# A two-layer hybrid decoder step on one core: norm sums taken token by token, a page-sum copy moved ahead of page issues, and attention heads with blocks turned one or two ahead of the scores

## What is computed

```python
def l2norm(x):
    xf = x.astype(jnp.float32)
    return xf * lax.rsqrt(jnp.sum(xf * xf, axis=-1, keepdims=True) + EPS)

# fox_prompt, for each block of 128 queries
s = jnp.einsum('bqhd,bkhd->bhqk', qi, k).astype(jnp.float32) * scale
s = s + ci[..., :, None] - cT[:, :, None, :]
s = jnp.where(kpos[None, :] <= qpos[:, None], s, -jnp.inf)
p = jax.nn.softmax(s, axis=-1).astype(v.dtype)
return jnp.einsum('bhqk,bkhd->bqhd', p, v)

# fox_sample: 2048 past tokens per sample, in 16 pages of 128
return (jnp.einsum('bhqk,bkhd->bqhd', p[..., :P], vp)
        + jnp.einsum('bhqk,bkhd->bqhd', p[..., P:], v))

# gdn_mix
c, conv_new = causal_conv(conv_in, conv_prev, conv_w)
c = jax.nn.silu(c)
q = l2norm(q.reshape(Bn, L, GDN_HEADS, GDN_DK)) * GDN_DK ** -0.5
k = l2norm(k.reshape(Bn, L, GDN_HEADS, GDN_DK))
...
o, S_new = run_chunks(gdn_chunk, S0.astype(jnp.float32), (q, k, v, g, beta), GDN_CHUNK)
o = rmsnorm(o, norm_g) * jax.nn.silu(z.reshape(...))
```

## Time and profile before

| | us |
|---|---|
| median of 3 runs | 2619.35 |
| lowest, highest | 2618.45, 2621.92 |
| the profiled execution's own time | 2619.68 |
| its span | 2617.9 |
| mean granted clock of TensorE, as a share of full speed | 0.977 |

### The profile page before, as it was taken

How to read it: one execution, slowest core, us unless ns; L and a number is a source line. 1 busy time by engine, 2 the same in 40 slices (tenths; PEclk the granted TensorE clock), 3 DMA queues, 4 the chain that set the end, 5 groups by cost and what they waited for, 6 DMA issues and landing times.

```text
span 2617.9 us, 53417 instructions
## 1 busy us (share of the span) xinstructions
PE 2497.5 (95%) x20047; PEld 2395.9 (92%) x20047; DVE 1269.6 (48%) x2225; ACT 566.7 (22%) x847; POOL 1682.8 (64%) x750
## 2 busy tenths in 40 slices
PE   7999998997789899999999999999999899999997
PEld 7999998995467799999999999999889799999996
DVE  4444335786333564443344443366766644444433
ACT  3222101004633222220022220022222221222101
POOL 5777775663411377777777777765545457777773
PEclk9999999998789899999999999999999999999998
DMA  4333334894375333333323333233333423333331
GB/s 125 90 89 96 101 79 113 285 308 131 84 220 188 85 89 95 89 88 99 118 81 89 95 91 100 82 91 100 116 116 98 126 81 88 89 95 90 96 93 61
DMA packets 472390, 291.19 MB, mean 111 GB/s; under 512 B 32785, under 2 KB 438411, under 8 KB 472270
## 3 DMA queue, kind: packets, MB, share of 16 engines
q1 hardware_dynamic: 407286, 221.15, 29.0%
q10 hardware_dynamic: 64992, 68.54, 8.4%
HBM read 273.50 MB, written 16.23 MB: 111 GB/s over the span
## 4 chain that ended last, share of the span: by engine, by line
PE 83%; DVE 8%; ACT 3%; issue 3%; DMA 1%; POOL 1%; ACTq 1%; DVEq 0%; SPq 0%; POOLq 0%
PE ACC L799 72%; PE ACC L1055 2%; PE ACC L1028 1%; DVE TB L2261 1%; DMA SSR<-in_state_ret_S 1%; DVE SSR L2178 1%; POOL WLO L708 1%; PE ACC L1306 0%; PE ACC L1296 0%; DVE XL L1736 0%; PE ACC L1122 0%; PE ACC L1037 0%; POOL WHI L705 0%; PE ACC L893 0%; PE ACC L1330 0%
## 5 line engine op out<-in xcount | busy, mean ns | idle before, releaser
L705 POOL TENSOR_TENSOR WHI<-RAW,ZERO 128x1024 fp32r<-128x1024 f32 (+1 forms) x341 | 693.0, 2032 | 677.2 <-PE ACC L799 640.3
L708 POOL TENSOR_TENSOR WLO<-RAW,WHI 128x1024 fp32r<-128x1024 f32 (+1 forms) x341 | 915.5, 2685 | 49.3 <-POOL WHI L705 2.3
L799 PE MATMUL ACC<-XH,WHI 128*128 128x260 f32 x4032 | 822.6, 285 | 4.3 <-DVE XL L1736 2.0
L799 PE MATMUL ACC<-XH,WLO 128*128 128x260 f32 x4032 | 813.7, 283 | 0.0
L799 PE MATMUL ACC<-XL,WHI 128*128 128x260 f32 x4032 | 812.4, 283 | 0.0
L799 PEld LDWEIGHTS ACC<-XH,WHI 128*128 128x128 f32 x4032 | 624.8, 189 | 22.9 <-issue 6.5
L799 PEld LDWEIGHTS ACC<-XH,WLO 128*128 128x128 f32 x4032 | 622.9, 189 | 0.0
L799 PEld LDWEIGHTS ACC<-XL,WHI 128*128 128x128 f32 x4032 | 621.6, 189 | 0.0
L799 PE MATMUL ACC<-HH,WHI 128*128 128x260 f32 x1408 | 284.2, 283 | 1.1 <-POOL WLO L708 1.1
L799 PE MATMUL ACC<-HH,WLO 128*128 128x260 f32 x1408 | 283.1, 282 | 0.0
L799 PE MATMUL ACC<-HL,WHI 128*128 128x260 f32 x1408 | 282.6, 282 | 0.0
(11 more groups left out here) (391 smaller groups left out, 2398.7 us busy)
## 6 DMA issues: line engine op xcount, KB each, us to landing
RAW<-in_ffn_w_gu SPq DMA_DIRECT2D x176, 512.0 KB, 3.9
RAW<-in_ffn_w_down SPq DMA_DIRECT2D x64, 704.0 KB, 4.8
KPAGES<-in_cache_fox_k ACTq DMA_DIRECT2D x128, 256.0 KB, 4.1
RAW<-in_c_w_in SPq DMA_DIRECT2D x48, 512.0 KB, 3.9
VPAGES<-in_cache_fox_v SPq DMA_DIRECT2D x72, 256.0 KB, 3.1
RAW<-in_ab_w_in SPq DMA_DIRECT2D x28, 512.0 KB, 5.4
VPAGES<-in_cache_fox_v ACTq DMA_DIRECT2D x56, 256.0 KB, 3.3
SSR<-in_state_ret_S ACTq DMA_DIRECT2D x8, 1024.0 KB, 5.4
```

Of the source, the lines that this page charges most:

```text
L705: pool.tensor_tensor(WHI[:, slot, 0:nk, :], RAW[:, slot, 0:nk, :], ZERO[:, :].broadcast_to([P, nk, P]), ALU.add).then_inc(hi_split, 1)
L708: pool.tensor_tensor(WLO[:, slot, 0:nk, :], RAW[:, slot, 0:nk, :], WHI[:, slot, 0:nk, :].bitcast(F32), ALU.subtract).then_inc(split, 1)
L799: ins = pe.matmul(ACC[acc][:, n, 0:HALF], w[:, slot, k, :], a[:, k0 + k, n * HALF:(n + 1) * HALF], start=first and opens, stop=final and c ...
```

## The change

1. **Attention heads.** Turns of blocks 0 and 1 of head h come before the first score of head h+1, and each later turn(h, q+2) right behind values(h, q), ahead of score(h+1, q+1). The turn of the next head's values into tokens (`vtok`) goes behind these turns. ACT takes both first turned blocks at once, takes exponents of two blocks together, puts exp(h, 3) into head h, and copies the value bank of head h only in head h+1, behind the next query copy; DVE's `lo` moves likewise. The four silus of the last head go behind all taps.
2. **Norm sums token by token.** The squares of a chunk of 128 tokens become the weights, and one column of ones is streamed: the sum of each token comes out on its own partition, in 5 columns a head (four chunks of 128 tokens and one that covers the last 128, 8 of them new). So there are 40 matmuls of one column for q and k, and 20 for the output norm. Root and reciprocal work on 128 x 20 or 128 x 40. `over_partitions` spreads them back with the column broadcast as weights against the identity: six matmuls for each of 8 (and 4) heads. `ROWSEL` goes. DVE squares q, ACT squares k in two parts; `SQH` lies elsewhere. Three of the four `values()` stand ahead of the sums.
3. **Page sum.** `value_sum(1)` stands ahead of `sample_gates()` and the page issue on ACT, and corner_xt(1) directly behind corner_xt(0) on PE.

```diff
@@ fox heads, PE
             for h in range(FOX_HEADS):
-                if 0 < h < FOX_HEADS - 1:
-                    fox_tokens(h + 1)
+                later = 0 < h < FOX_HEADS - 1
+                if later:
+                    fox_token_turn(h + 1, AB_K, "ktok")
+                fox_turn(h, 0)
+                fox_turn(h, 1)
+                if later:
+                    fox_token_turn(h + 1, AB_V, "vtok")
                 for q in range(NBLK):
-                    fox_turn(h, q)
                     if h + 1 < FOX_HEADS:
                         score(h + 1, q)
...
                     fox_values(h, q)
-
-            pe.wait_ge(fb_dve.sem, fb_dve.value("lo", FOX_HEADS - 1))
+                    if q + 2 < NBLK:
+                        fox_turn(h, q + 2)
+
@@ fox heads, ACT
             for h in range(FOX_HEADS):
-                if 0 < h < FOX_HEADS - 1:
-                    fox_query(h + 1)
-                    fox_keys(h + 1)
-                for q in range(NBLK):
-                    fox_turned(h, q)
-                    if h + 1 < FOX_HEADS:
-                        exponent(h + 1, q)
-                    if q < NBLK - 1:
-                        conv_taps(3 * h + q)
-                    if h == FOX_HEADS - 1:
-                        part = channels(GQ + 2 * q, 2)
-                        if q == 0:
-                            act.wait_ge(cs_pool.sem, cs_pool.value("a3"))
-                        act.wait_ge(cv_pool.sem, cv_pool.value("add3", 2 * q + 1))
-                        act.activation(part, part, ACT.Silu).then_inc(cv_act, 1)
-                await_step(act, fb_pe, "pv3", h)
-                fb_act.done(act.activation(MOH[:, h, 0:SEQ], bank(VALUE_BANK), ACT.Copy), "hi")
+                last = h == FOX_HEADS - 1
+                if h > 0:
+                    if not last:
+                        fox_query(h + 1)
+                    await_step(act, fb_pe, "pv3", h - 1)
+                    fb_act.done(act.activation(MOH[:, h - 1, 0:SEQ], bank(VALUE_BANK), ACT.Copy), "hi")
+                    if not last:
+                        fox_keys(h + 1)
+                fox_turned(h, 0)
+                fox_turned(h, 1)
+                if h > 0:
+                    exponent(h, 3)
+                conv_taps(3 * h)
+                fox_turned(h, 2)
+                if not last:
+                    exponent(h + 1, 0)
+                    exponent(h + 1, 1)
+                    conv_taps(3 * h + 1)
+                    fox_turned(h, 3)
+                    exponent(h + 1, 2)
+                    conv_taps(3 * h + 2)
+                else:
+                    fox_turned(h, 3)
+                    await_step(act, fb_pe, "pv3", h)
+                    fb_act.done(act.activation(MOH[:, h, 0:SEQ], bank(VALUE_BANK), ACT.Copy), "hi")
+                    conv_taps(3 * h + 1)
+                    conv_taps(3 * h + 2)
+                    for n in range(4):
+                        fox_silu(n)
@@ fox heads, DVE
+                if h > 0:
+                    await_step(dve, fb_act, "hi", h - 1)
+                    fb_dve.done(dve.tensor_tensor(MOL[:, h - 1, 0:SEQ], bank(VALUE_BANK), MOH[:, h - 1, 0:SEQ].bitcast(F32), ALU.subtract), "lo")
+                    if h + 1 < FOX_HEADS:
+                        fox_value_tokens(h + 1)
+                if h + 1 < FOX_HEADS:
+                    row_max(h + 1, 0)
                 normalize(h, 3)
                 if h + 1 < FOX_HEADS:
-                    if h > 0:
-                        fox_value_tokens(h + 1)
-                    row_max(h + 1, 0)
                     for q in range(1, NBLK):
                         row_max(h + 1, q)
                         normalize(h + 1, q - 1)
-                await_step(dve, fb_act, "hi", h)
-                fb_dve.done(dve.tensor_tensor(MOL[:, h, 0:SEQ], bank(VALUE_BANK), MOH[:, h, 0:SEQ].bitcast(F32), ALU.subtract), "lo")
-
             dve.memset(bank(7), 0.0).then_inc(v_clear, 1)
+            await_step(dve, fb_act, "hi", FOX_HEADS - 1)
+            last = FOX_HEADS - 1
+            fb_dve.done(dve.tensor_tensor(MOL[:, last, 0:SEQ], bank(VALUE_BANK), MOH[:, last, 0:SEQ].bitcast(F32), ALU.subtract), "lo")
@@ norms, PE
+            def token_sums(b, squares, j):
+                for c in range(CHUNKS):
+                    col = norm_column(c, j)
+                    ins = pe.matmul(bank(b)[:, col:col + 1], squares[:, j, chunk_tokens(c)], ONES[:, 0:1], start=True, stop=True)
+                return ins
+
+            def over_partitions(acc, j):
+                for c in range(NBLK):
+                    n, first = divmod(P * c, HALF)
+                    col = norm_column(c, j)
+                    left = RN[:, col:col + 1].broadcast_to([P, P])
+                    if first + P <= HALF:
+                        pe.matmul(acc[:, n, first:first + P], left, IDENT[:, :], start=True, stop=True)
...
+            for _ in range(V_SLOTS - 1):
+                values()
+            pe.wait_ge(ln_dve.sem, ln_dve.value("sqq"))
             for j in range(2 * GDN_HEADS):
-                r = j if j < GDN_HEADS else 32 + j - GDN_HEADS
-                pe.wait_ge(ln_act.sem, ln_act.value("sqq" if j < GDN_HEADS else "sqk"))
-                for n in range(2):
-                    ins = pe.matmul(ACC[0][0:NORM_ROWS, n, 0:HALF], row_select(r), SQH[:, j, n * HALF:(n + 1) * HALF],
-                                    start=j == 0, stop=j == 2 * GDN_HEADS - 1)
+                if j >= GDN_HEADS:
+                    pe.wait_ge(ln_act.sem, ln_act.value(f"sqk{(j - GDN_HEADS) // 2}"))
+                ins = token_sums(0, SQH, j)
             ln_pe.done(ins, "sum")
-            for _ in range(V_SLOTS):
-                values()
+            values()
+            pe.wait_ge(fb_dve.sem, fb_dve.value("lo", FOX_HEADS - 1))
             pe.wait_ge(ln_dve.sem, ln_dve.value("inv"))
@@ pair, PE
                 corner_xt(0)
+                corner_xt(1)
                 values()
-                corner_xt(1)
                 values()
@@ norms, ACT
-            ln_act.done(act.activation(SQH[:, 0:GDN_HEADS, :], channels(GQ, GDN_HEADS), ACT.Square), "sqq")
-            ln_act.done(act.activation(SQH[:, GDN_HEADS:, :], channels(GK, GDN_HEADS), ACT.Square), "sqk")
+            for n in range(2):
+                ln_act.done(act.activation(SQH[:, GDN_HEADS + 2 * n:GDN_HEADS + 2 * n + 2, :], channels(GK + 2 * n, 2), ACT.Square), f"sqk{n}")
+            act.wait_ge(ln_pe.sem, ln_pe.value("sum"))
+            half = CHUNKS * GDN_HEADS
+            for first, c, scale, name in ((0, 1, float(P), "stdq"), (half, 0, 1.0, "stdk")):
+                ln_act.done(act.activation(RN[:, first:first + half], bank(0)[:, first:first + half], ACT.Sqrt, bias=EPSC[:, c:c + 1], scale=scale), name)
...
-            act.wait_ge(ln_pe.sem, ln_pe.value("sum"))
@@ pair, ACT
                     if p == 0 and n == LEVELS - 1:
+                        value_sum(1)
                         sample_gates()
...
-                if p == 0:
-                    value_sum(1)
@@ last head and norms, DVE
+            dve.wait_ge(cv_act, 2)
+            q = PRJ[:, GQ:GQ + GDN_HEADS, :]
+            ln_dve.done(dve.tensor_tensor(SQH[:, 0:GDN_HEADS, :], q, q, ALU.mult), "sqq")
+
             dve.wait_ge(ln_act.sem, ln_act.value("stdk"))
-            ln_dve.done(dve.reciprocal(TA[0:NORM_ROWS, :], TA[0:NORM_ROWS, :]), "inv")
+            ln_dve.done(dve.reciprocal(RN, RN), "inv")
```

80 lines of the change are left out of this document (41 added, 39 removed).

## The result

The changed kernel is slower: 2629.66 us against 2622.06 (medians of 20 runs each), ratio 1.0026, 95% interval 1.0015 to 1.0038. A second comparison gave 1.0030 (1.0015 to 1.0044). The forecast was 2611.4 with a range of 2597 to 2623, so 8 us less than before; the kernel takes 7 us more (0.26%).

A forecast was written before the change was run, and what follows sets the result against it. TensorE (PE), busy 95% of the span, was taken as the bound, with only layer 0's mixer able to move. Heads with q and k -3.9, page sum -5.0, output norm +0.9 gave -8.0 us: 2611.4, range 2597 to 2623.

The forecast's parts named there:

- What bounds the kernel: Whole span: PE busy 95%, so outside layer 0's mixer only PE's work counts; the stretch 619 to 896 us can move.
- moves as a block: Everything behind layer 0's mixer: PE's own work, expected to shift as one with the -8.0 us.
- The heads: Attention heads: ACT becomes the bound at 12.9 us a head, so the sums of q and k begin 13.1 us earlier.
- Rival C: Attention heads gain only half as PE's clock falls in the gaps; 6.5 us missing, 2618 us; chance 0.13.
- Sums of q and k: Norm of q and k: 40 one-column matmuls at the low clock take 17.5 us against 9.94, 7.6 more.
- Rival A: Token sums run at 0.225 us each with the clock up, spreading saves 3.2 us; 2595.4 us; chance 0.13.
- The spreading of q and k: Norm of q and k: 7 matmuls at low clock, 41 at 0.23 us; 13.3 us against 8.6, 4.7 more.
- Rival B: Spreading of both norms stays at the low clock, costing 11.2 us more; 2622.6 us; chance 0.22.
- The output norm: Output norm: sums part 9.7 us against 9.12, spreading 8.4 against 8.07; together +0.9, bounds -5 and +4.
- The page sum: Pair 0: copying the page sum before the page issue removes PE's 4.46 us stall; -5.0 us, bounds 0 and 8.
- rival D: Page turn in pair 0 waits for its pages, so the page sum change gains nothing; 2616.4 us; chance 0.07.
- The sum: Whole kernel: -3.9 - 5.0 + 0.9 = -8.0 us on the profiled 2619.68, giving 2611.4 on the median's scale.

The follow-up runs named there:

- after_look4: The changed kernel run once more without any edit, for one more trace; 2632.17 us.
- after_look3: The changed kernel run a fourth time without any edit, for one more trace; 2632.62 us.
- heads_only: Kernel before with only the new head order and squares of q on DVE; norms by rows, four turns behind the sums, old page sum; 2611.89 us.
- out_undone: Changed kernel with the output norm alone put back to row sums and row spreading; 2620.81 us, ratio 0.9992 to the kernel before.
- warm_full: Changed kernel plus ten unused dense 512-column matmuls ahead of the q and k token sums; 2622.38 us, ratio 1.0006 to the kernel before.
- after: The changed kernel itself, all parts of the change in, against the kernel before; 2629.66 us against 2622.06, ratio 1.0026.
- heads_page: Changed kernel with both norms put back to row sums and row spreading, new head order and page sum kept; 2612.85 us, ratio 0.9971 to before.
- qk_undone: Changed kernel with the norm of q and k alone put back to row sums and row spreading; 2616.27 us, ratio 0.9979 to the kernel before.
- turns_behind2: Second run of turns_behind, nothing further changed; 2607.25 us.
- turns_behind: Changed kernel with both norms by rows and all four page turns behind the sums of q and k; 2604.57 us, ratio 0.9941 to before.
- rows_warm: turns_behind plus twelve unused dense 512-column matmuls ahead of the row sums; 2608.44 us, ratio 0.9939 to the kernel before.
- token_turns_behind: Changed kernel, norms still token by token, with all four page turns behind the token sums; 2628.3 us, ratio 1.0021 to the kernel before.
- page_only: Kernel before with only the page sum copied ahead of the page issue and the second corner ahead of the page turn; 2615.09 us, ratio 0.9978.
- experiment 3: Changed kernel with unused dense matmuls ahead of or among token sums, with turns behind them, or unedited; 2629.18, 2638.43, 2628.3 and 2632.62 us.
- spread_warm: Changed kernel plus three unused dense matmuls behind the last page turn, ahead of the q and k spreading; 2624.31 us, ratio 1.0004 to before.
- warm_among: Changed kernel plus five unused dense matmuls ahead of the token sums and one behind each head's five sums; 2638.43 us, ratio 1.0055 to before.
- norms_only: Kernel before with only both norm passes token by token; 2637.97 us, ratio 1.0060.

## Why the prediction was wrong, point by point

- **What bounds the kernel.** Right in the main: behind mixer 0 the large difference is in layer 1's waits, which both kernels have. But "moves as a block" was too strong: from landmark to landmark the traces differ by up to 13 us.
- **The heads.** Right in mechanism. ACT copied `MOH` at 635.68, 648.24 and 661.24, 12.6 and 13.0 us apart (forecast 12.9), and the last sits at 667.95. The first sums came 11.6 us earlier in the first trace, 9.5 and 8.9 in after_look4 and after_look3, against 13.1 on record. Term mis-sized by 1.5 to 4 us; in the first trace the squares could start 2.3 us later than forecast (677.09 against 674.8) and took 2.8 us for 3.6. heads_only gives this part alone -9.7 us. Rival C, half of the gain missing, is nearest in after_look3, with 4.2 of its 6.5 us.
- **Sums of q and k.** Right: 17.23 us at 0.50, forecast 17.5; 0.22 a sum at full clock, as on record (0.225). Rival A fell: it had the price at full clock right, but with the clock lifted ahead of it the pass still took 14.7 us, since the clock did not hold.
- **The spreading of q and k: the step that failed.** I let seven matmuls run at the low clock and 41 at the high one, "by the 128x128 rows", because the clock had risen 3.05 us into dense 128x128 work at 724.45. Four traces (after_look3, after_look4, out_undone, warm_full) show this spreading for 20.65 us, PE busy, at 0.50 from first to last: in them it did not lift the clock. In the first profile the rise came 1.5 us into it, behind the 1.89 us of a page turn. My 13.3 us was therefore one of two outcomes, 12.3 or 21.4 us with DVE's last product, and I had put all on the shorter. The two traces of after with the long one have a mean clock of 0.972 and 0.970, the three with the short one 0.974 to 0.976. The 38 times divide at the same place; if the clock marks the course in the runs without a trace too, it is 23 to 15 for the long one. That the first profile agrees with my working here is luck of the run. Rival B had the mechanism and the place. I gave it 0.22, and the row for it, 8.07 us at 0.50 in the output norm with PE busy, was in my own list; I set it aside because those matmuls read 64 rows.
- **The output norm.** Same step. Sums 8.69 (8.8), the spreading 10.4 us at 0.50 in all five traces of after, so from the first sum to the last product 20.7 us in place of 17.2: +3.5, against +0.9. The bound "+4, all low" was nearly the value.
- **A term that was missing.** "Three page turns ... come earlier; they were hidden and stay so." With row norms they were hidden behind root and reciprocal, and behind them the clock was at 1.00 when the spreading began. Moved ahead of the sums they leave PE to wait 4.04 us, and the spreading costs 14.2 us (heads_page, qk_undone) for 7.8 (before, heads_only, turns_behind2), 11.7 or 12.7 (turns_behind, rows_warm). heads_page against turns_behind puts that at 5 to 8 us by the ratios. In the changed kernel, where root and reciprocal are short, this term is not what failed: with the turns back behind the sums (token_turns_behind) the ratio is 1.0021 for 1.0026.
- **The page sum.** Right: -4.8 at its place, -5.8 by page_only's ratio, forecast -5.0. No page came late, so rival D fell.
- **The sum.** Forecast -8.0 on the profiled scale. In the first trace the output norm's sums start 9.7 us earlier (862.89 against 872.58), 0.8 more than the 8.9 on record: the 1.5 us missing in the heads had come back in the sums, the spreading and pair 0. The output norm then took 2.6 more than forecast, and 1.4 went at 890.36, where the output projection restarted after 3.66 us of waiting and met the low clock (first line), then recovered (second):

```profile
891.60:894.90 3.30, 3.30 (x17) 3.30 (x17) 0.00 (x0) 0.00 (x0) 0.00 (x0) 0.50 0.00 0
894.90:900.00 5.10, 5.10 (x44) 5.10 (x43) 3.88 (x3) 1.26 (x2) 4.57 (x2) 0.99 0.00 0
```

  That gives -8.0 - 0.8 + 2.6 + 1.4 = -4.8, for -4.6 at the landmark. The other course has 13 us more, as added up under experiment 3. Weighted 23 to 15 the landmark is about +3, and the rest of the measured +6.8 (by the ratio) is not accounted for: the profiled runs of after in the first course lie 3 us under the median of their group, and before's profiled run had the shortest layer 1. I leave that open.

The Trainium skill ("TensorE: Matmul & The Clock Gate", Part 1) describes the granted clock as following how busy the engine has been, full rate once it is kept busy. Where 512-column work ran unbroken (spread_warm, token_turns_behind) the traces agree; where 1-column sums or this spreading kept PE busy for 17.2 and 20.65 us at 0.50, they do not, and the measurement decides.

## What to carry to other kernels

Before narrow matmuls replace wide ones, ask what the clock does under them and behind them: a row of the trace with the same shape at the low clock and PE busy outweighs a rise seen under other work. Short independent work that stands between two dependent passes may be what keeps the clock up, so moving it elsewhere can cost more than it frees (heads_page against turns_behind). And where one profile disagrees with the median, compare the mean clock of all runs first, then profile again until both courses are seen.

## What the runs showed of the hardware

- The clock fell from 1.00 to 0.50 with PE busy: 2.75 us into 1-column sums that followed 8.85 us of dense work and 0.59 us of waiting (warm_full), and 1.5 and 2.9 us into row spreading (rows_warm, turns_behind).
- 29.2 us of sums with a 512-column matmul after every five never rose above 0.50 (warm_among).
- The token spreading (128x128, 128x4, 128x124, 128x8 columns in turn) ran at 1.00 for 10.8 to 10.9 us where the clock was up at its start (spread_warm, token_turns_behind, norms_only), and at 0.50 for 20.65 us where it was not (four traces); in the three others of after the clock rose 1.5 us into it. So the same instructions kept either level.
- PE's weight loads waited for layer 1's states 2 to 5 times an execution, 4.2 to 12.4 us in all, in kernels that have the same layer 1 (4.2 to 9.4 in five traces of after); that difference alone is larger than the effect under study.
